# One wait less ahead of the first PLE gate weights: a two-layer MoE and attention kernel on one core

## What is computed

```python
h = h + mix
h = h + hier_moe(rmsnorm(h, norm_ffn[i]), ...)                          # 512 rows x 1024, 32 experts, 2 of them for each row
gate = jax.nn.sigmoid(rmsnorm(h, norm_ple[i]) @ w_ple_gate[i] + b_ple_gate[i])
h = h + gate * (p[i] @ w_ple[i])
```

## Time and profile before

| | us |
|---|---|
| median of 3 runs | 1996.27 (1993.53 to 1997.13) |
| the profiled execution | 1998.46 |
| its span in the profile | 1996.7 |
| TensorE busy | 1928.7 (97%) |
| granted TensorE clock, mean over the span | 0.985 of full speed |

### The profile page before, as it was taken

The page is one execution under the profiler, slowest core; times in us unless marked ns, Lnnn a source line. Parts: engine busy times, 40 slices in busy tenths (PEclk is TensorE's granted clock), DMA queues, the critical chain, the costliest instruction groups (busy, mean ns, idle before and its releaser), DMA issues.

```text
span 1996.7 us, 21995 instructions
## 1 busy us (share of the span) xinstructions
PE 1928.7 (97%) x8606; PEld 1004.5 (50%) x8606; DVE 803.4 (40%) x2057; ACT 432.8 (22%) x883; POOL 88.0 (4%) x116
## 2 busy tenths in 40 slices
PE   8999999999999889999999999999988999999998
PEld 6886644444444335544454444444433564654555
DVE  4553454221111144455544422211114548874663
ACT  2000101011110024175210111111112532124453
POOL 0000000000000010023000000000001000000000
PEclk9999899999999899999999999999989999998999
DMA  7815489999999982121548999999999222120000
GB/s 308 196 70 228 166 337 405 428 428 428 427 427 429 422 342 101 57 85 42 231 169 352 412 429 426 429 428 429 427 421 354 83 90 77 52 84 1 12 12 22
DMA packets 49414, 512.32 MB, mean 257 GB/s; under 512 B 5392, under 2 KB 7568, under 8 KB 19344
## 3 DMA queue, kind: packets, MB, share of 16 engines
q1 hardware_dynamic: 40848, 480.86, 59.1%
q0 software_dynamic: 8448, 29.89, 3.9%
HBM read 484.38 MB, written 26.35 MB: 256 GB/s over the span
## 4 chain that ended last, share of the span: by engine, by line
PE 86%; DMA 6%; DVE 3%; ACT 2%; issue 2%; POOL 1%; SPq 0%; DVEq 0%; POOLq 0%; ACTq 0%
PE ps L1114 22%; PE ps L1158 10%; PE ps L1081 8%; PE ps L531 6%; PE ps L1979 6%; PE ps L737 5%; PE ps L1529 4%; PE ps L1696 3%; PE ps L2177 3%; PE ps L2314 3%; PE ps L1727 2%; DMA ring<-in_wexp 2%; PE ps L2332 2%; PE ps L2351 1%; DMA ring<-in_wall 1%
## 5 line engine op out<-in xcount | busy, mean ns | idle before, releaser
L1114 PE MATMUL ps<-ring,arena 128*48 128x512 f32 x1504 | 390.2, 606 | 25.1 <-issue 13.0
L1114 PEld LDWEIGHTS ps<-ring,arena 128*48 128x48 f32 x1504 | 114.8, 125 | 221.1 <-issue 219.6
L1127 DVE TENSOR_TENSOR arena<-arena,ps 48x512 f32<-48x512 f32 x64 | 44.2, 690 | 446.3 <-ACT arena L1121 446.2
L1081 PEld LDWEIGHTS ps<-arena,h 128*128 128x128 f32 x1024 | 158.6, 190 | 44.6 <-issue 44.6
L1158 PE MATMUL ps<-ring,arena 128*48 128x512 f32 x768 | 173.6, 593 | 2.8 <-DMA ring<-in_wexp 1.7
L1081 PE MATMUL ps<-arena,h 128*128 128x192 f32 (+1 forms) x1024 | 174.3, 325 | 0.0
L1114 PE MATMUL ps<-arena 128*48 128x512 f32 x544 | 172.7, 607 | 1.0 <-issue 1.0
L1121 ACT ACTIVATE arena<-ps 48x512 f32<-48x512 f32 x64 | 37.8, 590 | 460.3 <-PE ps L1114 460.3
L1979 PE MATMUL ps<-ring,arena 128*128 128x512 f32 (+3 forms) x384 | 132.7, 500 | 0.8 <-DVE arena L369 0.8
L1529 PE MATMUL ps<-ring,arena 128*128 128x512 f32 x256 | 112.7, 594 | 5.2 <-issue 4.2
L737 PE MATMUL ps<-ring,arena 128*128 128x512 f32 x256 | 112.8, 594 | 0.1
(11 more groups left out here) (301 smaller groups left out, 2315.7 us busy)
## 6 DMA issues: line engine op xcount, KB each, us to landing
ring<-in_wexp SPq DMA_DIRECT2D x136, 2048.0 KB, 19.6
arena<-in_wexp SPq DMA_DIRECT2D x50, 2048.0 KB, 16.1
ring<-in_wall SPq DMA_DIRECT2D x25, 2048.0 KB, 7.6
ring<-in_wexp SPq DMA_DIRECT2D x12, 1024.0 KB, 14.5
y_d<-arena POOLq DMA_DIRECT2D x60, 192.0 KB, 7.1
yo_d<-gbuf SPq DMA_DIRECT2D x2, 4032.0 KB, 46.3
ring<-in_wall SPq DMA_DIRECT2D x3, 1536.0 KB, 7.4
xs_d<-h POOLq DMA_DIRECT2D x8, 512.0 KB, 7.0
```

Of the source, the lines that this page charges most:

```text
L1081: mm = pe.matmul(banks[4 + t % 2][:, k * 4 * CAP + z0:(k + 1) * 4 * CAP], h[:, i, kk * P:(kk + 1) * P], RT["sel"][:, NT * (p_ % 2) + i, z0 ...
L1114: mm = pe.matmul(outs[m], xeT[:, e_ // 4 % 2, k, e_ % 4 * CAP:(e_ % 4 + 1) * CAP], ws[m][:, k, :], start=(k == 0), stop=(k == KT - 1))
L1127: dve.tensor_tensor(hh[0:CAP, e_ % 2, :], sl[0:CAP, e_ % 2, :], banks[1][64:64 + CAP, :], ALU.mult).then_inc(S["hh"], 1)
```

## The change

SP no longer waits for the second gather before it sends for the first unit of gate weights. What is left is the wait for the slot. Nothing else changes, in neither layer.

```diff
         def sp_ple(sp, l):
-            sp.wait_ge(*M("yg_1", l, 16))
             u = units[("ple", l, 0)]
             for name, v in u.before:
                 sp.wait_ge(S[name], v)
             half = UNIT // 2
             sp.dma_start(u.ap[:, 0:half], u.src[:, 0:half]).then_inc(S["ple_a"], 16)
             sp.dma_start(u.ap[:, half:], u.src[:, half:]).then_inc(S[f"ring{u.slot}"], 16)
             sp.wait_ge(*M("yg_7", l, 16))
             sp_load(sp, ("ple", l, 1))
```

## The result

| | before | after |
|---|---|---|
| median of 8 runs each, us | 1994.03 (1988.57 to 1997.13) | 2001.18 (1998.20 to 2004.24) |
| the profiled execution, us | 1998.46 | 1999.75 |
| its span, us | 1996.7 | 1998.0 |
| granted clock, mean | 0.985 | 0.987 |

The changed kernel takes 1.0038 times as long (95%: 1.0026 to 1.0050), 7.15 us more by the medians. Forecast were +5.5 us, and slower.

A forecast was written before the change was run, and what follows sets the result against it. TensorE, busy 1928.7 of 1996.7 us, was taken as the bound. Transfers +1.5 us plus clock 2 x 2.0 us gave +5.5 us on the median 1996.27: 2001.8 us, range 1995.5 to 2004.5.

The forecast's parts named there:

- Part 1: TensorE's stops before the first and third gate products go in both layers: at most 5.2 us gained.
- Part 2: Gate weights pass one for one beside gathers 0 and 1: 3.5 us more in layer 0, 3.4 in layer 1.
- Part 3: L1171 stands behind gather 1's addition on DVE: TensorE 3.5 and 3.2 us later; transfers alone +1.5 us.
- Part 4: The clock falls after TensorE's longer stop before the last two experts' product: 2.0 us per layer, 0 to 2.7.
- Faster: Rival: gather 1 less than 0.6 us later, early load pays, 4 to 5.2 us gained, 1991 to 1992.3; chance 0.09.
- Long turns: Rival: engines move one gather, then one half unit; gather 1 pays 2.5 us, total 1996 to 1998; chance 0.08.
- The clock stays up: Rival: same delay, clock stays up or falls in one layer only; +1.5 to +3.5 us; chance 0.19.
- nothing: Rival: SP is held elsewhere until the gathers are through, so the change does nothing; chance 0.05.
- Slower still: Rival: whole unit goes ahead of gather 1 (4.9 us), clock falls for longer; +9 us, 2005.3; chance 0.09.

The follow-up runs named there:

- e4: The changed kernel with five unused products ahead of TensorE's waits at the start of PLE; 1997.72 us, ratio 1.0023 to the kernel before.
- e5: The changed kernel with the unit loaded in four parts, rows of 4 KB instead of 8 KB; 1994.83 us, ratio 0.9997 to the kernel before.
- e12: The changed kernel with the unit loaded in one part, rows of 16 KB; 2001.36 us, ratio 1.0036 to the kernel before.
- e8: The changed kernel with L1171 between DVE's additions of gather 0 and gather 1; 1993.71 us, ratio 1.0001 to the kernel before.
- e3: The changed kernel loading only an eighth of each half of the first gate unit; 2071.28 us, layer 0 stretch 33.9 us.
- e1: The kernel before with SP's wait for gather 1 turned into one for gather 0; 1991.25 us, ratio 0.9994.
- e6: e1 with SP's wait before the second unit also one gather earlier (yg_6 for yg_7); 1990.64 us, ratio 0.9978 to the kernel before.
- e2: The changed kernel with SP waiting for gather 1 between the unit's halves, only the first half early; 1994.89 us, ratio 1.0001 to the kernel before.

## Why the prediction was right, and where its sizes were off

The predicted mechanism held: later gathers, a longer stop behind L1171, a fallen clock, and gates that are no longer late. That the time came so near (2001.2 for 2001.8 forecast) is luck. The forecast stood on a median of three runs, 1996.27 us; the eight runs have 1994.03, which is 2.2 us less. The change cost 7.15 us by the medians, 1.65 more than forecast, and the two errors largely cancel. The terms' own errors don't: all three point the same way. With the averages of the two profiles of each kernel:

| term, both layers, us | forecast | measured |
|---|---|---|
| gathers later, so TensorE's stop longer | +6.7 | +8.9 |
| stops before the gates gone | -5.2 | -4.1 |
| clock (from e4) | +4.0 | +4.3 |
| sum | +5.5 | +9.1 |
| the stretches themselves | | +8.3 |

The stop before the last rows was 1.4, 1.6, 1.6, 1.6 us before and 6.0, 6.4, 5.0, 6.5 after: 4.4 us more for each layer. The 0.8 us by which the three terms exceed the stretches are short pauses that went as well, such as one of 0.2 us within the first transposes and some around the gate products: from the first gate product to the third tile's transposes, less the stop on the second unit, it is 23.5, 23.5, 23.5 and 23.3 us before and 23.2 after. The runs themselves gave +7.15 and, in the repetition, +9.05 us by the medians, 1.0038 and 1.0036 by the ratios.

- **Part 1, the gain: right in kind, 5.2 us was one profile's figure.** The stops went completely, the ones on the second unit too. A repeat of the unedited kernel has 3.0 us of them. The prediction gave no range for this term, and that was the omission: the first stop of layer 0 was 2.4 us in one execution and 1.0 in the other.
- **Part 2, the delay: the step that failed in size.** Forecast were 3.5 and 3.4 us, by 182 and 176 new packets passing one for one. From the start of the last down product, gather 1 lands 2.9 and 2.8 us later before (2.9 and 2.9 in the repeat), and 7.6, 7.9, 6.5 and 8.1 us after: 4.6 us more. The turns were right as long as both queues had rows (e5, e12). Two things were not. The gathers start later, by 4.16 - 1.69 = 2.5 us in layer 0 and as much in layer 1, of which the prediction had nothing. And part of the unit is through before they start: from gather 0's first row to gather 1's landing the weights' queue moved 1.30 MB in layer 0 and 1.23 in layer 1, against 0.31 and 0.32 before, so 0.99 and 0.91 MB are new there (121 and 111 packets, not 182 and 176), 2.3 and 2.1 us at 427 GB/s. 2.5 + 2.3 = 4.8 and 2.5 + 2.1 = 4.6 us, near the 4.6 us measured on average (4.7 and 5.1 in this pair of profiles). Counted in bytes the two are one thing: during the later start the weights run on at the full rate, 1.76 MB in 4.15 us, and so get ahead. And the prediction's premise that the weights' queue never runs dry while the gathers run was wrong. The unit's last packet moves at 719.11 us, when gather 1 lands (719.17), and in layer 1 at 1518.03, before gather 1 does (1518.52). So the whole unit did go ahead of gather 1, and the bound that I had put down for that, 4.9 us, was nearly the result. In the repeat it did so in layer 1; in layer 0, where more weights (3.6 MB) were left at the start, the last of it came 1.6 us behind gather 1.
- **Part 3, who waits: right.** e8 takes L1171 from behind gather 1 and gets the loss back; e3 takes the bytes away and the delay goes with them.
- **Part 4, the clock: right, and about right in size.** It fell in both layers. e4, which keeps it up, puts the price at 4.3 us for 4.0 forecast (2.2 for 2.0 in each layer).
- **The rivals.** "Faster" fell: it asked for less than 0.6 us of delay. "Long turns" fell by the reports and the counts of rows in e5 and e12. The Trainium skill (DMA: Bandwidth & Descriptors, Queues, rings and completion order) has an engine drain a packet of some 9 to 17 descriptors before it turns to the next queue. The counts here speak for one row from each queue in turn. "The clock stays up" and "nothing" fell at the windows of both layers. "Slower still" was right in its premise: the unit went ahead of gather 1 in three of four layers, and the delay came near its 4.9 us. Its time, +9 us, was not reached by the first comparison (+7.15) nor by either ratio; it is what the repetition has by its medians (+9.05). The Trainium skill's rule on the same page (Rules for kernel authors) to issue a transfer early and wait for it late is true of the gate's own wait, which vanished; the cost came on another queue. e1 and e6 are early too, but behind gather 0, when the gathers' rows are already moving.

Left open: what makes the gathers' first rows 2.5 us later when the gate weights are queued, and from what amount on; why the layers of e5 differ by 1.7 us in gather 1, and why its runs don't show what its stretch does; and what makes the 17 us of slow clock near 1830 us come and go. Both profiles of the kernel before have these 17 us and neither of the change has. Whether the change has to do with that, and so whether the runs' difference has something of it in it, was not tested.

## What to carry to other kernels

A transfer that is moved earlier to hide its own wait costs something when it lies queued while another queue sends for data that the critical engine needs next. Price that first at all the bytes that then stand in front, at the rate that the trace shows (4.9 us here, against 4.6 measured); a price by turns of one row for one is right only while both queues have rows. Then look for the latest moment that still hides the early transfer (here behind gather 0), and take what does not need the late data out of its line (here L1171). Before stops of 1 to 2 us are booked as gain, look at a second profile of the same kernel.

## What the runs showed of the hardware

- Two queues on the same engines took turns by the row, whether the weights' rows were 4, 8 or 16 KB (50, 33 and 22 rows of a gather beside 49, 35 and 25 of weights in the first us, layer 0). With smaller weight rows the neighbour's first gather was through earlier at the same bytes (7.6 us instead of 8.6 to 9.2).
- A POOL transfer started 1.7 to 1.9 us behind its sending with 0.7 to 1.7 MB of weights left, and 3.6 to 3.8 us behind it amid the experts' loads, 4.1 to 4.3 us with 2.5 MB and more of weights left.
- Of the stops at this place, those of 3.8 to 6.5 us (the change twice, e2, e5, e12) were followed by a granted clock of 0.50 in part or all of the next 5 us, and those of 2.0 to 2.9 us (e4, e8) were not. That is what these rows show, with this work around them; it isn't a limit.
- The kernel before ran from 1825 to 1842 us at 0.50, with TensorE busy throughout: 83 matmuls of 205 ns, where the changed kernel's take 130 ns at 0.93. The 75 ns more are 6.2 us, about the 6.3 us by which the two pages' busy times differ, and as much as was to be measured. Five of the fourteen profiled executions have such 17 us there.
